# A hybrid decoder step on one core: another order of the prologue (root table, tile scaling, first weights, first projection)

## The chip, the cores and the metric

The kernel is one program on one core of a Trainium2 chip. The core has five engines that run their own instruction streams and meet at semaphores: TensorE (PE in the rows; PEld is its weight load), VectorE (DVE), ScalarE (ACT), GpSimd (POOL) and SyncE (SP), which here only issues transfers. The metric is the device time of one execution in microseconds (us), as the median of several runs.

## The reference, cut to what matters

One inference step of a one-layer decoder on 512 prompt tokens and 8 sample tokens, all in fp32. What the first microseconds of the kernel compute is this:

```python
h = rmsnorm(x, norm_mix_pre)          # x * rsqrt(mean(x*x) + EPS) * g, D_MODEL = 1024
z = einsum('btd,de->bte', h, w_in)    # queries, K/V of three branches, gates, S5 input u, merge gates
q, kv, gn, u, gm = split(z)
dt = exp(s5_log_dt); a_bar = exp((s5_a_re + 1j * s5_a_im) * dt)      # per S5 group and state
b_bar = ((a_bar - 1) / lam) * b_c                                    # then a scan over time with a_bar
```

The rest of the layer (sparse attention over a paged cache, the S5 recurrence, merge, MLP) follows and is the same in both kernels.

## The kernel before, in words

The tokens form four tiles of 128 rows and one of 8 (tile index 4, TT in the code), 520 columns in all once transposed (NT), handled in halves of 260 (HALF). The normalised input is kept transposed in hT, as 8 blocks of 128 channels by 520 tokens.

**SyncE** issues, in this order, the identity part of the constants (L726), the four prompt tiles of 512 KB (L728), the sample rows (L729), the rest of the constants (L730, 303 KB) and then the stream plan: slab 0 is w_in's 512 columns of the S5 input, 2 MB in one transfer (L784), followed by small_loads (L734 to L738: s5_d, s5_b_glu, the page table), then slab 1 in eight transfers (L803), state_load (L743) which waits until all five tiles are scaled, slab 2, and so on. A slab buffer is one of three.

**ScalarE** first issues five small loads (L1021 to L1024: the S5 parameters, then the two gain vectors), spreads log_dt over a tile (L1026), takes the exponential of dt (L1029), and then for each of the five token tiles does a Square with a row sum (L1016) and a Sqrt (L1009). Exp, Sin and Sin of the S5 angles follow (L1035 to L1037), then the loads of the C matrices (L1040) and a long zero fill (L1042).

**TensorE** transposes the S5 parameters and the gains, then in norm_transposes (through tp, L2153) each scaled tile in two halves of four 128-column blocks, into four PSUM banks in turn. It waits until all ten half tiles are evacuated (`xnt_free` at 10) and starts the units of the projection. A gemm unit (L2175) is one block of 128 output channels: for each half of the tokens, 8 matmuls of 260 columns. An fp32 matmul shows as two instructions, so a unit has 32. Units alternate between two pairs of PSUM banks, and ScalarE evacuates them (L1085). The order of the units is fixed in HEAD_UNITS and REST_UNITS: u0, u1, two of transposed C matrices ("ct"), u2, "kk", "ft" and "kt" units of S5, u3, q6, h0, then `chunk_ends(0)` (L2287), q7, and so on. chunk_ends(0) waits for `tables_done`, for ScalarE's chunk copies, and for the pair_free of the "ft" units.

**VectorE** copies parameters and gains out of PSUM, computes the S5 angle (L1451 to L1458), which ends with `ang_ready`, and then in input_norm takes for each tile the reciprocal of the root (L1436), scales the tile (L1439) into one of two buffers, and evacuates the transposes of the tile before with the gain multiplied in (L1429). After the last evacuation it waits for `trig_ready` from ScalarE and computes the S5 tables: L1461 to L1478 (a_bar and the coefficient of B), L1493 to L1500 (B with powers, `bb_ready`), L1513 to L1518 (tables of powers by doubling), and raises `tables_done` after the last L1518.

**GpSimd** zero-fills two areas (L874, L875), issues four small loads of the B matrices (L878), waits for `unit_ready` from VectorE, and computes powers of a_bar and products with C from there on.

## Time and profile before

| what | value |
|---|---|
| median of 3 runs | 1288.23 us (1286.51 to 1292.34) |
| the profiled execution's own time | 1290.65 us |
| its span, first to last instruction | 1288.9 us |
| mean granted TensorE clock | 0.983 of full |
| busy TensorE, weight load, VectorE, ScalarE, GpSimd | 95%, 78%, 64%, 24%, 26% |
| HBM read, written | 159.29 MB, 13.84 MB |

All views are of one profiled execution; times are microseconds from the first instruction. In a timeline, a row has the start, the length, the engine, the line of the kernel, the operation, out<-in, how many were merged, and in brackets the idle time ahead of it and what released it. Rows of the issuing queues (SPq, ACTq) are the time of the issue, not of the transfer. In the table of stretches, a row has from:to, its length, then busy us and count of instructions of PE, PEld, DVE, ACT and POOL in that order, then the granted TensorE clock (1.00 is full), the DMA share and GB/s. In the table of groups, a row has count, busy us, mean ns of one, and idle time before. DMA rows end with the median us from issue to landing.

### The profile page before, as it was taken

How to read it: one execution, taken by the hardware profiler on the slowest of the kernel's cores; microseconds unless marked ns; L12 is line 12 of the kernel's file. 1: busy time of each engine (PE TensorE's matmuls, PEld its weight loads, DVE VectorE, ACT ScalarE, POOL GpSimd, SP SyncE). 2: the span in 40 equal slices, each digit the busy share in tenths (PEclk: the TensorE clock that was granted, in tenths of full speed). 3: DMA queues.
4: the chain of work that ended last, by engine and by line, in shares of the span. 5: the costliest groups of instructions: out<-in, count | busy, mean ns of one | idle time of the engine just before them, and what ended most of it. 6: DMA issues, size and time to landing. Idle time of an engine off the chain costs nothing.

```text
span 1288.9 us, 20454 instructions
## 1 busy us (share of the span) xinstructions
PE 1226.6 (95%) x7778; PEld 1003.0 (78%) x7778; DVE 825.0 (64%) x1376; ACT 307.2 (24%) x728; POOL 337.9 (26%) x404
## 2 busy tenths in 40 slices
PE   5999899999999789999999999998999999999997
PEld 4888776668887556656788888887888888888886
DVE  6997332227888777877766554776664565467455
ACT  5485110120010465556311111132000000000002
POOL 5943224312221032223112111000211212513540
PEclk9999998899999999999999999998999999999999
DMA  9234445537777344434661322420231131131101
GB/s 256 50 132 135 164 110 173 163 108 311 261 261 258 114 117 135 157 97 151 221 203 66 114 78 103 177 103 17 74 122 66 66 131 66 66 131 66 66 1 67
DMA packets 122097, 166.09 MB, mean 129 GB/s; under 512 B 36448, under 2 KB 90528, under 8 KB 117648
## 3 DMA queue, kind: packets, MB, share of 16 engines
q1 hardware_dynamic: 103408, 104.72, 25.7%
q0 software_dynamic: 8080, 50.58, 10.9%
q10 hardware_dynamic: 10512, 9.49, 2.2%
q8 instruction: 62, 1.02, 0.3%
q14 instruction: 35, 0.29, 0.1%
HBM read 159.29 MB, written 13.84 MB: 134 GB/s over the span
## 4 chain that ended last, share of the span: by engine, by line
PE 86%; DVE 8%; ACT 3%; issue 2%; another core or an unknown queue 1%; DMA 0%; POOL 0%; ACTq 0%; DVEq 0%
PE PS L2623 47%; PE PS L2175 14%; PE PS L2352 9%; PE PS L2153 4%; PE PS L2304 2%; PE PS L2469 2%; PE PS L2501 2%; DVE small L1843 2%; PE PS L2534 1%; DVE PS L1841 1%; DVE R L1863 1%; ACT KVU L1136 1%; PE PS L2331 1%; PE PS L2287 1%
## 5 line engine op out<-in xcount | busy, mean ns | idle before, releaser
L2175 PE MATMUL PS<-hT,stream 128*128 128x260 f32 (+1 forms) x800 | 187.4, 395 | 5.1 <-ACT QO L1085 3.6
L2175 PEld LDWEIGHTS PS<-hT,stream 128*128 128x128 f32 (+1 forms) x800 | 153.2, 194 | 37.1 <-issue 4.9
L2623 PE MATMUL PS<-R,stream 128*128 128x260 f32 x752 | 173.5, 382 | 0.0
L2623 PEld LDWEIGHTS PS<-R,stream 128*128 128x128 f32 x752 | 142.8, 190 | 21.9
L2623 PE MATMUL PS<-R 128*128 128x260 f32 x592 | 135.7, 383 | 0.0
L2623 PEld LDWEIGHTS PS<-R 128*128 128x128 f32 x592 | 112.1, 190 | 17.8 <-DVE R L1895 0.8
L2352 PE MATMUL PS<-R 128*128 128x256 f32 (+1 forms) x544 | 119.0, 379 | 3.8 <-DVE R L1667 2.4
L2352 PEld LDWEIGHTS PS<-R 128*128 128x128 f32 x544 | 101.4, 194 | 18.5 <-DVE R L1667 2.8
L2623 PE MATMUL PS<-R,QO 128*128 128x260 f32 x496 | 113.8, 383 | 1.4 <-DVE QO L1895 1.4
L1983 DVE TENSOR_TENSOR R<-PS,R 128x260 f32<-128x260 f32 x100 | 42.4, 426 | 102.8 <-PE PS L2623 101.6
L2623 PEld LDWEIGHTS PS<-R,QO 128*128 128x128 f32 x496 | 93.8, 190 | 16.8 <-DVE QO L1895 2.2
L1983 DVE TENSOR_TENSOR KVU<-PS,KVU 128x260 f32<-128x260 f32 x92 | 39.2, 426 | 95.3 <-PE PS L2623 88.2
L2623 PE MATMUL PS<-hT,stream 128*128 128x260 f32 (+2 forms) x408 | 98.1, 384 | 0.6 <-ACT R L1290 0.6
L1667 DVE STREAM_TRANSPOSE R<-stream 128x2048 f32<-128x2048 f32 (+1 forms) x34 | 75.2, 2233 | 19.5 <-PE PS L2304 9.8
L2623 PEld LDWEIGHTS PS<-hT,stream 128*128 128x128 f32 x408 | 77.5, 196 | 12.4 <-ACT R L1290 0.8
L936 POOL DMA_INDIRECT R<-in_cache_kv_slc,row_kv x56 | 54.1, 966 | 110.3 <-DVE R L1619 65.9
L1619 DVE STREAM_TRANSPOSE R<-R 128x2048 f32<-128x2048 f32 x14 | 32.0, 2302 | 79.0 <-PE PS L2304 78.1
L2153 PEld LDWEIGHTS PS<-consts,R 128*128 128x128 f32 (+3 forms) x465 | 50.4, 141 | 40.8 <-issue 33.4
L1330 ACT ACTIVATE R<-PS 128x260 f32<-128x260 f32 x50 | 19.4, 388 | 251.2 <-PE PS L2623 251.2
L710 POOL TENSOR_SCALAR R<-R,small 128x512 f32<-128x512 f32 (+3 forms) x64 | 48.3, 758 | 116.6 <-DVE small L1850 116.6
L2153 PE MATMUL PS<-consts,R 128*128 128x128 f32 (+3 forms) x465 | 64.6, 279 | 11.9 <-DVE R L1863 7.2
L1273 ACT ACTIVATE R<-PS,small 128x512 f32<-128x512 f32 (+3 forms) x128 | 66.0, 527 | 9.2 <-DVE small L1843 8.3
(450 smaller groups left out, 1864.5 us busy)
## 6 DMA issues: line engine op xcount, KB each, us to landing
stream<-in_cache_kv_slc SPq DMA_DIRECT2D x128, 128.0 KB, 2.1
stream<-in_w_mlp_up SPq DMA_DIRECT2D x8, 2048.0 KB, 7.9
stream<-in_w_mlp_down SPq DMA_DIRECT2D x8, 2048.0 KB, 7.9
stream<-in_w_in SPq DMA_DIRECT2D x4, 2048.0 KB, 9.4
stream<-in_state_kv_win SPq DMA_DIRECT2D x16, 512.0 KB, 6.0
stream<-in_w_in SPq DMA_DIRECT2D x8, 1024.0 KB, 7.9
out_kv_win_sample<-in_state_kv_win POOLq DMA_DIRECT2D x1, 8176.0 KB, 43.3
R<-in_cache_kv_slc SPq DMA_DIRECT2D x56, 128.0 KB
```

The costliest lines, as they stand in the source:

```text
L710: return eng.tensor_scalar(S, S, ainv[:, k:k + 1], gtm[:, t, col:col + 1], ALU.mult, ALU.mult)
L936: pool.indirect_dma_start(key_pages(k)[:, x, :], None, slc_rows, bass.IndirectOffsetOnAxis(ap=row_kv[:, at:at + 1], axis=0)).then_inc(keys ...
L1273: ins = nc.scalar.activation(PP[:, n % 2, j, c0:c0 + P * (t + 1)], score_block(n, j, c0), ACT.Exp, bias=amx[:, k:k + 1], accum_out=asm[:, ...
L1619: V.transpose(KT[k % 2], KL[key_buffer(k)]).then_inc(kt_ready, 1)
L1667: V.transpose(ROWST[:, w % 3, 0:256 * ns].rearrange("p (s x) -> p s x", x=256), slab(s)[:, 0:512 * ns].rearrange("p (s k x) -> p k s x", k ...
L1843: V.reduce_max(amx[:, k:k + 2 * nx], S[:, :, 0:P * (t + 1)], AX, negate=True).then_inc(as_max, 1)
L1983: V.tensor_tensor(to, product_of(w, i), other, ALU.add).then_inc(pr_added, 1)
L2153: return nc.tensor.transpose(out, in_, ident[0:rows, 0:rows])
L2175: ins = M(pair(u)[0:w, hf, 0:HALF], lhs[k], rhs[k][:, HALF * hf:HALF * hf + HALF], start=(k == 0), stop=(k == n - 1))
L2304: ins = M(PS[32 * g:32 * g + 32, 4 + a4, cols], QM[rows, 256 * b + c0:256 * b + c0 + 32], keys[rows, :, c0:c0 + 32], start=(k == 0 and dh ...
L2352: ins = M(out, w1c[:, kind, x, :], rhs, start=(x == 0), stop=(x == 7))
L2623: ins = M(product_of(w, i)[:, c0:c1], lhs[:, k, :], rhs[:, k, c0:c1], start=(k == 0), stop=(k == nk - 1))
```

## The change

Five things change, all ahead of the second unit of the projection. The load of the Sqrt table and the root of tile 0 come ahead of the S5 parameters, and the gain vectors' loads ahead of the parameters'. GpSimd scales tiles 1, 3 and 4, VectorE keeps 0 and 2; the reciprocals stay on VectorE. Slab 0 comes in two transfers of 256 of its 512 columns, and the first is issued once tile 0 has landed, ahead of the rest of the constants. TensorE does the first unit, u0, in parts: the first 256 token columns (tiles 0 and 1) in two halves of the contraction, one ahead of the transposes of tile 3 and one ahead of those of tile 4, and the rest when all tiles are evacuated; the low half of the token columns is 260 wide, so four columns come by themselves. VectorE's S5 angle moves behind the evacuation of tile 2.

```diff
         def _(sp):
...
             sp.dma_start(xtm[0:NB, TT, :], a["x_sample"].rearrange("b o d -> (b o) d")).then_inc(x_in[TT], 16)
+            sp.wait_ge(x_in[0], 16)
+            sp.dma_start(slab(0).rearrange("p (k c) -> p k c", c=512)[:, :, 0:256],
+                         a["w_in"].rearrange("(k p) c -> p k c", p=P)[:, :, C_U:C_U + 256]).then_inc(x_in[0], 16)
             sp.dma_start(consts[:, P:CO_N], a["consts"][:, P:CO_N]).then_inc(masks_in, 16)
...
             def state_load():
-                sp.wait_ge(xn_ready, TT + 1)
+                sp.wait_ge(xn_ready, 2)
+                sp.wait_ge(xg_ready, 3)
...
-                    sp.dma_start(S[:, 0:KD * w].rearrange("p (k c) -> p k c", c=w),
-                                 wq[:, :, c0:c0 + w]).then_inc(done, 16)
+                    c1 = 256 if n == 0 else 0
+                    sp.dma_start(S[:, 0:KD * w].rearrange("p (k c) -> p k c", c=w)[:, :, c1:w],
+                                 wq[:, :, c0 + c1:c0 + w]).then_inc(done, 16)
...
         def _(pool):
...
+            for k, t in enumerate((1, 3, TT)):
+                r = ROWS[t]
+                pool.wait_ge(gains_ready, 2 + k)
+                if t >= 2:
+                    pool.wait_ge(xnt_full, 2 * (t - 1))
+                nc.gpsimd.tensor_scalar(xn[0:r, t % 2, :], xtm[0:r, t, :], rstd[0:r, t:t + 1], None,
+                                        ALU.mult).then_inc(xg_ready, 1)
             pool.wait_ge(unit_ready, 1)
...
         def _(act):
...
+            for w, name in enumerate(("norm_mix_pre", "norm_mlp_pre")):
+                act.dma_start(gnat[KD * w:KD * w + KD, :], a[name].rearrange("(k p) -> k p", p=P)).then_inc(gains_in, 16)
             for k, name in enumerate(("s5_a_re", "s5_a_im")):
                 act.dma_start(nat[:, k, :], a[name].rearrange("(i g) n -> i (g n)", g=2)).then_inc(par_in, 16)
             act.dma_start(ldt2, a["s5_log_dt"].rearrange("(i g) -> i g", g=2)).then_inc(par_in, 16)
-            for w, name in enumerate(("norm_mix_pre", "norm_mlp_pre")):
-                act.dma_start(gnat[KD * w:KD * w + KD, :], a[name].rearrange("(k p) -> k p", p=P)).then_inc(gains_in, 16)
+            act.wait_ge(eps_ready, 1)
+            nc.scalar.activation(preload, epsb, ACT.Sqrt)
+            input_root(0)
             act.wait_ge(par_in, 16 * N_PAR)
             nc.scalar.activation(nat[:, 2, :].rearrange("p (g n) -> p g n", g=2),
                                  ldt2.unsqueeze(2).to_broadcast([NST, 2, N5]), ACT.Copy).then_inc(nat_ready, 1)
+            for t in range(1, TT + 1):
+                input_root(t)
             act.wait_ge(par_ready, 1)
             nc.scalar.activation(dt, ldt, ACT.Exp).then_inc(ldt_ready, 1)
-            act.wait_ge(eps_ready, 1)
-            input_roots()
...
         def _(dve):
...
-            dve.wait_ge(par_full, 1)
-            V.tensor_copy(par3, PS[:, 0, 0:3 * NST]).then_inc(par_ready, 1)
             dve.wait_ge(gains_full, 1)
             V.tensor_copy(gflat, PS[:, 1, 0:2 * KD]).then_inc(gains_ready, 1)
             dve.wait_ge(gains_ready, 1)
+            norm_scale(0)
+            norm_inverse(1).then_inc(gains_ready, 1)
+            dve.wait_ge(par_full, 1)
+            V.tensor_copy(par3, PS[:, 0, 0:3 * NST]).then_inc(par_ready, 1)
+            norm_evac(0)
+            norm_scale(2)
+            norm_inverse(3).then_inc(gains_ready, 1)
+            norm_evac(1)
+            norm_inverse(TT).then_inc(gains_ready, 1)
+            norm_evac(2)
             dve.wait_ge(ldt_ready, 1)
             V.tensor_tensor(mag, are, dt, ALU.mult)
...
             V.tensor_scalar(ang2, ang2, 3.1415925, -3.1415925, ALU.min, ALU.max).then_inc(ang_ready, 1)
-            input_norm()
+            norm_evac(3)
+            norm_evac(TT)
             dve.wait_ge(trig_ready, 1)
...
+            def first_unit(part):
+
+                S = slab(0).rearrange("p (k c) -> p k c", c=512)
+                bank = pair(0)[:, 0, :]
+                if part < 2:
+                    for k in range(4 * part, 4 * part + 4):
+                        M(bank[:, 0:2 * P], S[:, k, 0:P], hT[:, k, 0:2 * P], start=(k == 0), stop=(k == KD - 1))
+                    return
+                for k in range(KD):
+                    M(bank[:, 2 * P:HALF], S[:, k, 0:P], hT[:, k, 2 * P:HALF], start=(k == 0), stop=(k == KD - 1))
+                for k in range(KD):
+                    ins = M(pair(0)[:, 1, 0:HALF], S[:, k, 0:P], hT[:, k, HALF:NT], start=(k == 0), stop=(k == KD - 1))
+                ins.then_inc(pair_full, 1)
+
             pe.wait_ge(consts_in, 16)
+            pe.wait_ge(gains_in, 32)
+            tp(PS[:, 1, 0:2 * KD], gnat, 2 * KD).then_inc(gains_full, 1)
+            norm_transposes(0)
             pe.wait_ge(par_in, 16 * N_PAR)
...
             ins.then_inc(par_full, 1)
-            pe.wait_ge(gains_in, 32)
-            tp(PS[:, 1, 0:2 * KD], gnat, 2 * KD).then_inc(gains_full, 1)
-            norm_transposes()
+            norm_transposes(1)
+            norm_transposes(2)
+            pe.wait_ge(xnt_free, 4)
+            pe.wait_ge(x_in[0], 32)
+            first_unit(0)
+            norm_transposes(3)
+            first_unit(1)
+            norm_transposes(TT)
             pe.wait_ge(xnt_free, 10)
+            first_unit(2)
...
-                    wait_slab(pe, n)
+                    if to != ("u", 1):
+                        wait_slab(pe, n)
...
             for u, unit in enumerate(UNITS):
-                projection(u, unit)
+                if u:
+                    projection(u, unit)
```

norm_transposes(t) is the body of the old loop for one tile, with xn_ready for tiles 0 and 2 and xg_ready for 1, 3 and 4. norm_scale(t) is norm_inverse(t) and the old scaling. A later wait on xn_ready (L2648) counts 3 fewer.

## Rows read from the trace of the kernel before

**Rows 1.** The page: busy time and share of TensorE.

```profile
PE 1226.6 (95%) x7778; PEld 1003.0 (78%) x7778; DVE 825.0 (64%) x1376; ACT 307.2 (24%) x728; POOL 337.9 (26%) x404
```

**Rows 2.** Timeline of TensorE, 0 to 160 us.

```profile
8.45 0.28 PE L2153 MATMUL PS<-consts,QO 16*128 16x16 f32 x1 [0.82 <-DMA QO<-in_norm_mlp_pre]
...
17.47 1.09 PE L2153 MATMUL PS<-consts,QO 128*128 128x128 f32 x8 [0.96 <-DVE QO L1439]
...
20.90 15.98 PE L2175 MATMUL PS<-hT,stream 128*128 128x260 f32 x64 [0.73 <-DVE hT L1429]
...
70.14 3.71 PE L2287 MATMUL PS<-QO,R 128*128 128x136 f32 x16 [2.43 <-issue]
...
144.20 15.98 PE L2175 MATMUL PS<-hT,stream 128*128 128x260 f32 x64 [3.56 <-ACT QO L1085]
```

**Rows 3.** Timeline of VectorE, from 11 and from 69 us.

```profile
11.00 0.75 DVE L1439 TENSOR_SCALAR QO<-KVU,small 128x1024 f32<-128x1024 f32 x1
...
20.77 0.15 DVE L1461 TENSOR_TENSOR small<-small 128x16 f32<-128x16 f32 x1
...
69.27 0.68 DVE L1518 TENSOR_TENSOR R<-R,KVU 128x512 f32<-128x512 f32 x1
```

**Rows 4.** Table of stretches (columns as told above).

```profile
10.50:11.00 0.50, 0.00 (x0) 0.00 (x0) 0.16 (x2) 0.50 (x2) 0.00 (x0) 1.00 0.95 180
...
20.77:69.95 49.18, 45.28 (x270) 38.21 (x270) 46.96 (x119) 23.36 (x30) 43.59 (x90) 0.97 0.51 130
...
22.30:25.70 3.40, 3.40 (x9) 2.67 (x8) 2.96 (x20) 2.70 (x1) 2.63 (x13) 0.50 1.18 263
...
70.20:73.50 3.30, 3.30 (x15) 3.30 (x16) 2.70 (x6) 3.23 (x6) 2.17 (x3) 0.51 0.16 52
...
145.20:148.40 3.20, 3.20 (x9) 2.52 (x8) 2.97 (x18) 0.00 (x0) 0.00 (x0) 0.50 1.00 348
```

**Rows 5.** Timeline of ScalarE.

```profile
8.03 1.04 ACT L1016 ACTIVATE QO<-KVU 128x1024 f32<-128x1024 f32 x1
...
9.18 1.28 ACT L1009 ACT_TABLE_LOAD   x1
...
17.77 1.28 ACT L1036 ACT_TABLE_LOAD   x1
...
29.90 0.60 ACT L1085 ACTIVATE KVU<-PS 128x520 f32<-128x520 f32 x1 [4.91 <-PE PS L2175]
...
143.54 0.60 ACT L1085 ACTIVATE QO<-PS 128x520 f32<-128x520 f32 x1 [9.71 <-remote]
```

**Rows 6.** Timeline of SyncE's queue, 0 to 40 us.

```profile
1.20 1.84 SPq L728 DMA_DIRECT2D KVU<-in_x_prompt  x4
...
4.50 0.46 SPq L784 DMA_DIRECT2D stream<-in_w_in  x1
...
16.57 10.30 SPq L803 DMA_DIRECT2D stream<-in_w_in  x8
```

**Rows 7.** DMA issues: first prompt tile, fourth, rest of constants, slab 0.

```profile
KVU<-in_x_prompt SPq DMA_DIRECT2D x1, 512.0 KB, 5.1
...
KVU<-in_x_prompt SPq DMA_DIRECT2D x1, 512.0 KB, 9.4
...
consts<-in_consts SPq DMA_DIRECT2D x1, 303.0 KB, 10.6
...
stream<-in_w_in SPq DMA_DIRECT2D x1, 2048.0 KB, 15.3
```

**Rows 8.** Groups by shape: GpSimd's scaling, narrow and 256-column matmuls.

```profile
L710 POOL TENSOR_SCALAR R<-R,small 128x512 f32<-128x512 f32 x16 | 16.6, 1041 | 38.3 <-DVE small L1850 38.3
...
L710 POOL TENSOR_SCALAR R<-R,small 128x128 f32<-128x128 f32 x16 | 7.6, 484 | 16.0 <-DVE small L1850 16.0
...
L2352 PE MATMUL PS<-R 128*128 128x256 f32 x512 | 113.7, 381 | 2.7 <-DVE R L1667 2.4
...
L2623 PE MATMUL PS<-hT,stream 128*128 128x4 f32 x24 | 3.2, 263 | 0.0
```

More of the change, by code:

```diff
@@ L288, in build @@
         xn_ready = sem("xn_ready")
+        xg_ready = sem("xg_ready")
         xnt_full = sem("xnt_full")
@@ L861, in build @@
         N_PAR = 3
-        NORM_UNITS = [(t, half) for t in range(5) for half in range(2)]
         @block.gpsimd
@@ L1010, in root, with input_root @@
                                             bias=epsb[0:rows, :])
-            def input_roots():
-                for t, r in enumerate(ROWS):
-                    act.wait_ge(x_in[t], 16)
-                    link(nc.scalar.activation(junk[0:r, :], xtm[0:r, t, :], ACT.Square,
-                                              accum_out=ssq[0:r, t:t + 1]))
-                    root(t, t + 1, r).then_inc(root_ready, 1)
+            def input_root(t):
+                r = ROWS[t]
+                act.wait_ge(x_in[t], 16)
+                link(nc.scalar.activation(junk[0:r, :], xtm[0:r, t, :], ACT.Square,
+                                          accum_out=ssq[0:r, t:t + 1]))
+                root(t, t + 1, r).then_inc(root_ready, 1)
+            for w, name in enumerate(("norm_mix_pre", "norm_mlp_pre")):
+                act.dma_start(gnat[KD * w:KD * w + KD, :], a[name].rearrange("(k p) -> k p", p=P)).then_inc(gains_in, 16)
             for k, name in enumerate(("s5_a_re", "s5_a_im")):
@@ L2153, in tp, with norm_transposes @@
                 return nc.tensor.transpose(out, in_, ident[0:rows, 0:rows])
-            def norm_transposes():
-                for v, (t, half) in enumerate(NORM_UNITS):
-                    r = ROWS[t]
-                    pe.wait_ge(xn_ready, t + 1)
+            def norm_transposes(t):
+                r = ROWS[t]
+                if t in (0, 2):
+                    pe.wait_ge(xn_ready, 1 + t // 2)
+                else:
+                    pe.wait_ge(xg_ready, 1 + t // 2)
+                for half in range(2):
+                    v = 2 * t + half
                     if v >= 4:
@@ L2647, in norm_back @@
                 r, k0 = ROWS[t], (XN_AT[t] - 6) % 2
-                pe.wait_ge(xn_ready, XN_AT[t])
+                pe.wait_ge(xn_ready, XN_AT[t] - 3)
                 if t == TT:
```

38 lines of the change are left out of this document (18 added, 20 removed).

## The prediction

> **What bounds the kernel now.** I read the page first [rows 1]: TensorE (PE) is busy 95% of 1288.9 us, so a change of the start is worth what it shifts the later TensorE work, and no more. Then the order of TensorE's work [rows 2]: the first projection (channel tile u0) starts at 20.90, having waited 0.73 us for VectorE (DVE), and from there PE is almost solid until it sits idle for 2.43 us before 70.14 (so from 67.71). That idle decides the case. What starts at 70.14 is L2287, the first chunk_ends, which waits for tables_done; the view names no releaser ("issue"), but VectorE's order does [rows 3]: the last L1518 of the S5 tables runs from 69.27 to 69.95 and the increment follows it. Going back, this table chain starts at L1461 at 20.77, the instant the last norm evacuation (L1429) is over, and VectorE is busy 46.96 of the 49.18 us between [rows 4]. So two chains run from about 20.8 to 70.1: TensorE's, with 2.43 us of slack, and VectorE's, with none. After 70.14 TensorE never waits long again before 140.7; 144.20 has a wait of 3.56 us [rows 2] whose cause the trace doesn't name.
>
> An earlier start of TensorE alone is therefore worth nothing: it lengthens the 2.43 us. What counts is when VectorE can begin L1461.
>
> **The change, part by part.**
>
> Roots. Before, the first Square waits behind the parameter path and the Sqrt table load stands between it and its root: 8.03, load 9.18 for 1.28, first root finished 10.76 [rows 5]. Now the load runs right after the five DMA issues (about 3.05 to 4.4, under the wait for data; the load lasts the same 1.28). Tile 0 lands at 1.20 + 5.1 = 6.3 [rows 6, 7], Square 1.04 and its accumulator read 0.2, Sqrt 0.3: root 0 at 7.9, 2.9 us sooner. The parameter copy waits for the last of ScalarE's five small loads, 8.45 before [rows 2], then root 1 at 10.1, root 2 at 11.5. Tile 3 lands at 2.6 + 9.4 = 12.0 [rows 7], so root 3 is at 13.4 and the last at 14.7. Exp's table load and the exponential of dt follow: 16.2. One load of 1.28 goes, on an engine that isn't late: nothing.
>
> Scaling. VectorE's is 0.75 a tile [rows 3]. GpSimd's isn't shown at 1024 columns; its two-operation form takes 484 ns at 128 and 1041 at 512 [rows 8]: slope 1.45 ns a column, so 1.8 us at 1024. Bounds: 0.75 (VectorE's) and 2.1 (twice the 512). I take 1.8. GpSimd has nothing else queued before unit_ready but its four load issues, over before root 1. Tile 1: reciprocal 10.3, ready 12.2. Tile 2 on VectorE: 13.9. Tile 3: from 14.1, ready 15.9. Tile 4 follows: 17.8. Cover: TensorE, as next shown, isn't ready for tile 3 before 18.3 and for tile 4 before 21.1. If GpSimd took 2.4 us more a tile, tile 3 would begin to cost. The Trainium skill (GPSIMD Engine Reference, Engine selection) advises against elementwise work there, but puts one-input work at roughly line rate; an estimate by it is 0.9 us a tile at that page's 1.2 GHz. By either price the sum is the same.
>
> First weights. The whole slab was issued at 4.50 and landed at 19.8 [rows 6, 7]. Its first half is now issued once tile 0 is in (6.4). In the queue it stands where the 303 KB of constants stood, which landed at 4.11 + 10.6 = 14.7. So by 14.7 some 0.3 MB are in; 2.1 MB then took 5.1 us (0.41 MB/us), the other 0.75 MB take 1.8: first half in at 16.5. Bounds: 15.5, where it no longer matters since tile 1's evacuation ends there, and 19.8. The rest lands near 20, before it is needed. SP's issues behind it (s5_d, s5_b_glu, page table, the next slab at 16.57 [rows 6]) go back by 2.7 us. That slab, the vectors and the page table are first read by q6 behind u3, by VectorE's L1507 and by its L1547 behind the tables, each over 15 us after landing: nothing. The state load's wait (both scaling semaphores) is met by 17.8, sooner than SP reaches it. The c loads on ScalarE's queue move 1 us back and are needed only when u0 and u1 are through: nothing.
>
> TensorE, from 16.5. first_unit(0): 8 instructions (an fp32 matmul is two) of 256 columns at 0.222 [rows 8]: 1.8, to 18.3. Eight transposes of tile 3, 1.1 [rows 2]: 19.4. first_unit(1), 1.8: 21.2. Tile 4's transposes 0.7 and VectorE's two small evacuations 0.2: xnt_free is complete at 22.1. Then 16 instructions of 4 columns at 133 ns [rows 8] = 2.1, work that the old unit didn't have, and 16 of 260, 3.5: u0 ends at 27.7 at full clock. Before, it ended at 29.9 [rows 5].
>
> Clock. Each time that dense work follows a sparse stretch the granted clock is 0.50 (1.2 of 2.4 GHz) for over 3 us: 22.3 to 25.7, 70.1 to 73.5, 145.2 to 148.4 [rows 4]. It costs 1.7 us each time, and it came 0 to 1.4 us after the dense work began. The new dense work begins at 16.5, so the dip falls in first_unit(0) and (1), and the evacuations are complete at 23.8, u0 at 29.4. Without it, 22.1 and 27.7. I take it inside, by those three rows.
>
> VectorE. The angle chain now stands behind evacuation 2 (17.0): 1.4 us for its seven small operations gives 18.4. ScalarE's Exp, Sin load 1.28 and two Sins follow (before, 17.77 to 19.38 for the load and Sins) [rows 5]: trig ready 20.4. But norm_evac(3) and norm_evac(4) come before the trig wait in VectorE's order, and these wait for transposes which TensorE has put behind first_unit(0) and (1). So **a wait takes the removed one's place**: L1461's successor starts not at 20.77 but at 23.8. The late party is the first weights.
>
> **Sum.** VectorE's chain +3.0, carried rigidly (its waits in between are on GpSimd, which starts from the same unit_ready): tables_done at 73.1. TensorE gets there at 67.2, 0.5 sooner, and sits idle 5.9 instead of 2.43 us. The half-clock stretch behind it costs 1.85 as before. ScalarE's table copies and chunk copies move with VectorE's chain. All later work moves by +3.0: 1290.65 of the profiled execution would be 1293.7. That execution stands 2.4 above the median 1288.23, so against the median: **1291.2 us**. Bounds: the first half in by 15.5 and no dip, 21.1, is +0.3; landing at 19.8 with the dip is +6.3.
>
> **Rivals.**
> (a) The new wait is short: half slab by 15.5, dip missing or behind the evacuations. Shift 0.3 to 1.3, TensorE 1 to 3 us sooner at 67.7 and that wasted: 1288.5 to 1289.5. For it: between 10.5 and 11.0 all queues together moved only 180 GB/s [rows 4], with GpSimd's small loads among them; should these interleave less with SP's queue, the half is in sooner. Against: their order is not changed. A gain past 0 has no room in this case, since trig itself is ready at 20.4.
> (b) The unexplained 3.56 us at 144.20, with its dip of 1.7, goes or shrinks since everything before has moved: 1291.2 - 5.3 = 1285.9. For it: ScalarE resumes at 143.54 [rows 5] for an evacuation whose matmuls ended at 140.2, so it isn't a plain dependence. Against: it may move along.
> (c) Slower beyond the measurable: the first half slab lands where the whole one did or later (it is cut into 1 KB rows rather than 2 KB, and its issue waits for tile 0). Place: TensorE's wait for x_in[0] = 32; price: one us for each us behind 16.5. From 19.9 on the loss is over 6.4: 1294.7.
> (d) The split doesn't do what it says: u0 ends no sooner, since 2.1 us of narrow matmuls and the dip eat the start. That is nearly in the forecast, same time.
> The Trainium skill (SBUF — State Buffer, two separate sides) says that GpSimd and a VectorE operation with two SBUF inputs lock each other out. By it tile 4's scaling until 17.8 would hold the angle chain by up to 0.8, trig 21.2. That is hidden in the forecast; it would take case (a)'s lower end from 0.3 to 0.5.
>
> **How the numbers follow.** A measurement of this kernel tells about 0.5%, 6.4 us, from no change. Forecast and (d) 0.57, (a) 0.20, (b) 0.12, (c) 0.08; the rest 0.03 for a gain that I don't see. Faster needs under 1281.8: the rest and a little of (b), 0.04. Slower needs over 1294.7: (c) and a new unexplained wait, 0.08. Same 0.88. The range takes in (b) at 1285.5 and the forecast's own bounds to 1295.
>
> **What would show it.** Right: root 0 near 7.9; first L-line of the projection at 16 to 17, u0's evacuation near 29; the S5 chain's first operation (before L1461) at 22 to 24; the idle before the first chunk_ends 4 to 7 us and that start at 71.5 to 74; clock 0.50 between 16.5 and 23. Wrong: S5 chain begun before 20.8, chunk_ends before 70, or the projection begun before 15.

## The result, and the profile after

| | before | changed |
|---|---|---|
| median | 1290.76 us (1282.97 to 1294.03, 9 runs) | 1297.43 us (1289.77 to 1301.15, 9 runs) |
| ratio of the two | | 1.0051, 95% interval 1.0027 to 1.0075 |
| the profiled execution | 1290.65 us, span 1288.9 | 1301.15 us, span 1299.4 |
| mean granted clock of it | 0.983 | 0.977 |

The changed kernel is slower by 6.6 us (3.5 to 9.7, from the interval), where 1291.2 and a shift of +3.0 were forecast. Its 1297.43 lies outside the range on the slow side. The median of the kernel before is 2.5 higher here than the 1288.23 of three runs that the forecast stood on; from 1290.76 the same shift gives 1293.8, still 3.6 short. The lines of the page and the timelines of TensorE, GpSimd and VectorE in the changed kernel's prologue (a row: start, length, engine, line, operation, out<-in, and in brackets the idle time ahead and its releaser):

```profile
span 1299.4 us, 20485 instructions
PE 1236.4 (95%) x7794; PEld 1012.1 (78%) x7794; DVE 824.2 (63%) x1373; ACT 306.5 (24%) x728; POOL 347.0 (27%) x407
```

```profile
12.88 3.68 PE L2177 MATMUL PS<-consts,QO 128*128 128x128 f32 x16 [1.89 <-POOL QO L891]
16.63 2.69 PE L2219 MATMUL PS<-hT,stream 128*128 128x256 f32 x8
19.15 1.04 PE L2177 MATMUL PS<-consts,QO 128*128 128x128 f32 x8
20.03 1.89 PE L2219 MATMUL PS<-hT,stream 128*128 128x256 f32 x8
21.85 0.66 PE L2177 MATMUL PS<-consts,QO 8*128 8x8 f32 x8
22.79 1.95 PE L2222 MATMUL PS<-hT,stream 128*128 128x4 f32 x16 [0.28 <-DVE hT L1442]
24.59 5.44 PE L2224 MATMUL PS<-hT,stream 128*128 128x260 f32 x16
```

```profile
9.97 2.85 POOL L891 TENSOR_SCALAR QO<-KVU,small 128x1024 f32<-128x1024 f32 x1 [1.01 <-DVE small L1451]
15.03 5.65 POOL L891 TENSOR_SCALAR QO<-KVU,small 128x1024 f32<-128x1024 f32 x2 [2.21 <-PE PS L2177]
```

```profile
17.20 0.17 DVE L1474 TENSOR_TENSOR small<-small 128x16 f32<-128x16 f32 x1
...
17.93 1.05 DVE L1478 TENSOR_SCALAR small<-small 128x16 f32<-128x16 f32 x1
...
22.30 0.44 DVE L1442 TENSOR_TENSOR hT<-PS,small 128x32 f32<-128x32 f32 x2 [1.22 <-PE PS L2177]
22.65 0.17 DVE L1485 TENSOR_TENSOR small<-small 128x16 f32<-128x16 f32 x1
```

These rows show the replaced wait. L1485 is the operation that was L1461, and it starts at 22.65 where it started at 20.77 [rows 3], straight behind the two small evacuations of tile 4 (L1442), which waited 1.22 us for transposes that stand behind both parts of the first unit. That is 1.88 us, and it is carried from there. TensorE's later stops in the changed kernel, and ScalarE's evacuations that released two of them ("remote" stands where the profile finds no instruction that ended just before the signal):

```profile
72.07 3.36 PE L2339 MATMUL PS<-QO,R 128*128 128x136 f32 x16 [4.19 <-DVEq L1565]
...
120.81 8.79 PE L2203 MATMUL PS<-hT,stream 128*128 128x260 f32 x32 [2.63 <-ACT QO L1100]
...
150.41 9.85 PE L2203 MATMUL PS<-hT,stream 128*128 128x260 f32 x36 [3.56 <-ACT QO L1100]
```

```profile
120.15 0.60 ACT L1100 ACTIVATE QO<-PS 128x520 f32<-128x520 f32 x1 [8.93 <-remote]
...
149.76 0.60 ACT L1100 ACTIVATE QO<-PS 128x520 f32<-128x520 f32 x1 [9.72 <-remote]
```

The first chunk_ends (72.07, before 70.14 [rows 2]) is 1.93 later. The stop at 150.41 is that of 144.20 [rows 2], 6.2 later and the same 3.56 long. Between them lies the stop at 120.81, which the kernel before does not have: ScalarE begins at 120.15 to evacuate a unit whose last matmul ended near 115.4 (TensorE's next group, L2306, starts at 115.23), so the unit's `pair_full` reached it nearly 5 us late. 1.93 of the shift thus comes from the prologue and 4.3 from this stop (2.63) and the half-clock stretch behind it (1.7). Together 6.2, against 6.6 measured. The two profiled executions differ by more, 10.5, and what they differ by over 6.2 comes behind 250. It goes with the clock: (1 - clock) x span is 29.9 us in the changed one and 21.9 in the other, and 0.977 is on the low side of that kernel's runs.

### The profile page after: what moved, and what is told of

It is laid out like the page before. It is cut to its first block, busy times and chain, and to the rows that moved or that the text cites. A ratio compares the mean times of both kernels' runs of the same rounds, so it can differ in the third digit from the quotient of the medians.

```text
span 1299.4 us, 20485 instructions
## 1 busy us (share of the span) xinstructions
PE 1236.4 (95%) x7794; PEld 1012.1 (78%) x7794; DVE 824.2 (63%) x1373; ACT 306.5 (24%) x728; POOL 347.0 (27%) x407
## 4 chain that ended last, share of the span: by engine, by line
PE 82%; DVE 10%; ACT 3%; issue 2%; another core or an unknown queue 1%; POOL 1%; DMA 0%; ACTq 0%; DVEq 0%
PE PS L2676 46%; PE PS L2203 10%; PE PS L2405 9%; PE PS L2177 5%; PE PS L2356 2%; PE PS L2522 2%; PE PS L2554 2%; DVE small L1867 2%; PE PS L2587 1%; ACT KVU L1151 1%; DVE PS L1865 1%; DVE R L1887 1%; PE PS L2384 1%; PE PS L2559 1%
## 5 line engine op out<-in xcount | busy, mean ns | idle before, releaser
L2203 PE MATMUL PS<-hT,stream 128*128 128x260 f32 (+1 forms) x768 | 180.4, 395 | 7.0 <-ACT QO L1100 6.2
L2203 PEld LDWEIGHTS PS<-hT,stream 128*128 128x128 f32 (+1 forms) x768 | 147.4, 194 | 38.2 <-ACT QO L1100 6.7
L2676 PEld LDWEIGHTS PS<-R,stream 128*128 128x128 f32 x752 | 142.8, 190 | 21.9
L2405 PE MATMUL PS<-R 128*128 128x256 f32 (+1 forms) x544 | 121.9, 386 | 4.4 <-DVE R L1691 2.4
```

What stands on the lines that cost most here:

```text
L2203: ins = M(pair(u)[0:w, hf, 0:HALF], lhs[k], rhs[k][:, HALF * hf:HALF * hf + HALF], start=(k == 0), stop=(k == n - 1))
L2405: ins = M(out, w1c[:, kind, x, :], rhs, start=(x == 0), stop=(x == 7))
L2676: ins = M(product_of(w, i)[:, c0:c1], lhs[:, k, :], rhs[:, k, c0:c1], start=(k == 0), stop=(k == nk - 1))
```

## The experiments

Ratios are to the kernel before on the same chip in the same minutes, and "by the ratio" means the ratio times that kernel's median; it can differ from the difference of the medians by up to 2.4 us. The "offset" at a place is how much later TensorE starts a piece of work than in the profiled execution before. The experiments ran on different chips: on one the kernel before takes 1289 us (chip A; e1, e2, e6, e7 and e13 to e16), on others 1264 (chips B: e3, e4, e5, e8 to e12, e17, e18). The first measurement, at 1290.76, looks like A, and its two traces have the late signals of A.

**VectorE alone late (e1), TensorE's program alone longer (e2).**

```diff
# e1: the kernel before, behind input_norm()
+            for _ in range(2):
+                link(V.memset(junk, 0.0))
# e2: the kernel before, behind pe.wait_ge(xnt_free, 10)
+            for k in range(KD):
+                M(pair(0)[:, 0, 0:4], ident, hT[:, k, 0:4], start=(k == 0), stop=(k == KD - 1))
```

> The kernel before, with nothing changed but VectorE's S5 table chain, which two memsets of an unused 128x1024 area (about 0.9 us each) hold back by 1.9 us, as the change did (22.65 against 20.77). Theory A: the whole measured loss is this delay, in two steps. The first chunk_ends moves from 70.14 to 72.0 (+1.9); and since TensorE's work then stands about 2 us later against the GpSimd gathers and SyncE's key issues, the late signal behind the pair evacuated near 118 now stops TensorE (idle 2 to 3 us and a half-clock stretch), so that the offset behind 124 is +5 to +7 and the time +6 us. Theory B (the second step comes from TensorE's 16 added instructions or from something else in the changed prologue): offset +1.9 at 72 and still +1.9 at 124, time +2 us, no idle of TensorE above 1 us near 120. Theory C (the second step is chance of one execution): the same as B in most executions.

> The kernel before, with 8 matmuls of 4 columns (16 instructions, about 2 us; what they write is overwritten) on TensorE right ahead of the first unit of the projection. TensorE has 2.43 us of idle ahead of 70.14, so the first chunk_ends stays at 70.1 with 0.4 us of idle ahead of it. Theory A (only a shift of the work behind 70 against GpSimd's gathers counts): offset 0 everywhere behind 70, time +0 (within 1 us). Theory B (the place of TensorE's code in its fetches, 16 instructions further as in the changed kernel, makes the late signal near 118 stop TensorE): chunk_ends at 70.1, and a new idle of 2 to 3 us near 118 to 120 with its half-clock stretch, offset +4 behind 124, time +4 us.

Measured: e1 1292.22 against 1289.09, ratio 1.0017 (0.9999 to 1.0035), which is +2.2 us with 0 just inside the interval. e2 1288.24, ratio 0.9993 (0.9971 to 1.0015). TensorE's first chunk_ends and the late signal in e1:

```profile
71.97 3.96 PE L2289 MATMUL PS<-QO,R 128*128 128x136 f32 x16 [3.85 <-issue]
```

```profile
116.24 0.61 ACT L1085 ACTIVATE QO<-PS 128x520 f32<-128x520 f32 x1 [4.18 <-PE PS L2177]
121.30 4.45 ACT L1136 ACTIVATE KVU<-PS 32x512 f32<-32x512 f32 x4 [4.45 <-remote]
```

So the first step is shown: VectorE's delay alone moves chunk_ends by 1.8. The second is not what theory A said. The projection unit is evacuated on time (116.24), the next signal, of a short unit, is late, and nobody on TensorE waits for it: no stop near 120. In e2 there is none either. So neither the delay nor the longer program brings the stop by itself, and theory A, which put the whole loss on the delay, fell.

How large the first step is, one pair of traces can't tell. The prologue of the kernel before varies by some 1.3 us between executions: without added work on VectorE its table chain starts at 19.46 to 20.77 in six traces (before, e2, e7, e10, e16, e17), and the 20.77 that all is measured from is the latest. The changed kernel's starts at 21.70 to 22.65 in six (changed, e6, e9, e11, e13, e14). The means, 19.96 and 22.10, are 2.1 apart, where the one pair gives 1.9.

**GpSimd's gathers taken away early on (e7 before, e6 changed; again in e16).** The same edit in each, with VectorE's waits to match:

```diff
-                    for x in range(0, 8, 2):
+                    for x in (range(8) if k < 7 else range(0, 8, 2)):
...
-            for k in range(NKU):
+            for k in range(7, NKU):
                 wait_key_buffer(pool, k)
```

> The kernel before, with the key pages of key units 0 to 6 all fetched by SyncE's direct loads (8 issues a unit in place of 4), so that GpSimd's first gathers come only with key unit 7. Theory A with its cause (signals of TensorE reach ScalarE late while GpSimd's gathers and SyncE's issues run against each other): no wait of ScalarE of over 3 us put down to a remote signal between 105 and 150 where its matmuls were long over; the 3.56 us idle of TensorE at 144.20 and its half-clock stretch (1.7 us) gone, so about 5 us sooner behind 150, time -5 us, if SyncE's loads keep up with VectorE. Rival: the late signals come from SyncE's issues or from TensorE's own instruction fetch, and stay: time 0 or slower, if the keys come late.

> The changed kernel, with the same shift of the key pages of units 0 to 6 from GpSimd's gathers to SyncE's direct loads. Theory A with its cause: both late signals (ScalarE waiting until 120.15 and until 149.76 for matmuls long over) are gone; TensorE's offset to the kernel before stays +1.9 from 72 to the end, less what the wait at 144 gave: against the same edit on the kernel before +2 us and not +6.6, time about 1288. Rival (the gathers are not the cause): the stop at 120.8 stays, and the time is that of the changed kernel, 1297, or more.

Measured: e7 1282.48, ratio 0.9945 (0.9922 to 0.9968); e6 1287.43, ratio 0.9969 (0.9943 to 0.9994). Neither trace has a late signal; in e7 the evacuation that waited until 143.54 [rows 5] follows its matmuls at once:

```profile
137.61 0.60 ACT L1085 ACTIVATE QO<-PS 128x520 f32<-128x520 f32 x1 [6.41 <-PE PS L2176]
```

That settles that on chip A the late signals come with GpSimd's gathers of key pages (8 in a row from about 107, 12 from about 127, one each 1.25 us): SyncE's loads alone, now twice as many, hold nothing. But the changed kernel, so treated, is still slower than the kernel before, so treated: by 3.1 us by the ratios, by 4.95 by the medians. The times can't tell that from my "+2"; the traces can. The projection unit that starts at 138.27 in e7 starts at 141.88 in e6, 3.6 later. 1.93 of it is the first chunk_ends. The rest is clock: ahead of chunk_ends TensorE is idle 2.46 us in e7 and 4.19 in e6; the group of 16 takes 2.09 in the one and 3.73, at half clock, in the other:

```profile
69.33 2.09 PE L2288 MATMUL PS<-QO,R 128*128 128x136 f32 x16 [2.46 <-issue]
```

```profile
71.26 3.73 PE L2340 MATMUL PS<-QO,R 128*128 128x136 f32 x16 [4.19 <-DVEq L1565]
```

**Both delays (e8), and the parts of the change taken back (e3, e4, e5).** e8 has the edits of e1 and e2. e3 is the changed kernel with the first unit whole:

```diff
-            pe.wait_ge(xnt_free, 4)
-            pe.wait_ge(x_in[0], 32)
-            first_unit(0)
             norm_transposes(3)
-            first_unit(1)
             norm_transposes(TT)
             pe.wait_ge(xnt_free, 10)
-            first_unit(2)
+            pe.wait_ge(x_in[0], 32)
+            wait_slab(pe, 0)
+            gemm(0, ...).then_inc(pair_full, 1)
```

e4 is the changed kernel with GpSimd's loop over (1, 3, TT) gone and `norm_scale(1)`, `norm_scale(3)`, `norm_scale(TT)` on VectorE in the places of `norm_inverse`; there the last one stands behind norm_evac(2). e5 has both edits.

> The kernel before with both earlier edits: VectorE's table chain held back by 1.9 us, and 16 narrow instructions more on TensorE ahead of the first unit. Theory D (the second step of the loss needs both: the shift of 1.9 us against GpSimd's gathers and a program of TensorE that is longer ahead of them, which puts its instruction fetch near 116 right behind the end of a unit whose signal is then late): chunk_ends at 72, a unit's evacuation near 120 that waits for a remote signal for 8 to 9 us, TensorE idle 2 to 3 us there, offset about +6 behind 124, time +6 us. Rival E (it is neither of these two but something else in the changed kernel, or chance): offset +2 behind 124, time +2 to +3, as with the delay alone (1292.22 against 1289.09).

> The changed kernel, but the first unit is one piece again behind all transposes (32 instructions, no 4-column matmuls). GpSimd's scaling of tile 4, over at 20.7, is then what VectorE waits for: its table chain starts at 22.0 (22.65 in the changed kernel, 20.77 before), chunk_ends at 71.3. Theory D: TensorE's program is as long as before ahead of the gathers, so no second stop near 120; offset +1.2 from 72 on, time +1 to +2 us against the kernel before. Rival E: a shift of over 1 us is enough: second stop near 120, offset +5, time +5 or more. If the interleave alone made the first step of the loss, the table chain would start at 20.8 instead.

> The changed kernel, but VectorE scales all five tiles and GpSimd none; the interleaved first unit stays. TensorE is solid from the landing of the first half slab (16.6) to the transposes of tile 4 (22.5), so the table chain starts at 22.3 to 22.7 as in the changed kernel (22.65), chunk_ends at 71.7 to 72.1: the interleave is by itself enough for the first step. Theory D: the second stop near 120 comes too, time +5 to +7 against before. Rival: GpSimd's slow scaling (2.83 us a tile) makes the delay; then the chain starts at 21 or sooner, chunk_ends at 70.2, time +0.

> The changed kernel with both taken back: VectorE scales all tiles, and the first unit is one piece behind all transposes. What is left of the change is the root table first, the split slab and the order of the small loads. Roots 3 and 4 end at 12.5 and 13.9, so all evacuations end by 19; the angle chain (1.4 us), one table load (1.28) and two Sins then set the start of the table chain: 20.5 to 21.0, against 20.77 before. chunk_ends at 69.9 to 70.4, no second stop near 120, time -1 to +1 us against before. If it came out at +2 us or more, a part that I hold harmless (the split slab, the order of the loads) costs something.

These came on a chip B, where the kernel before takes 1264.06 and no trace has a late signal, so they say nothing of the stop near 120. They measure the first step. The table puts them beside e10 and e11, the two kernels unchanged on another chip B. Its last column but one is the time from the start of the first chunk_ends to the start of the projection unit near 140, between which TensorE is almost never idle:

| kernel | table chain starts | idle, then length of the first chunk_ends | from there to the unit near 140 | median; ratio |
|---|---|---|---|---|
| e10, before | 19.84 | 2.75; 2.65 | 70.66 | 1264.20; 1.0006 (0.9990 to 1.0022) |
| e5, neither | 20.21 | 1.70; 2.09 | 68.95 | 1264.58; 1.0005 (0.9989 to 1.0020) |
| e4, VectorE scales | 20.98 | 5.87; 3.97 | 71.49 | 1269.84; 1.0038 (1.0018 to 1.0057) |
| e3, no interleave | 21.87 | 1.31; 2.09 | 68.93 | 1266.70; 1.0008 (0.9992 to 1.0024) |
| e11, changed | 21.78 | 4.15; 3.47 | 70.63 | 1268.71; 1.0032 (1.0015 to 1.0050) |
| e8, both delays | 21.98 | 1.68; 2.09 | 68.94 | 1267.86; 1.0028 (1.0012 to 1.0045) |

Each part is by itself enough for a delay of the table chain, against e10: the interleave (e4) for 1.1 us, GpSimd's scaling (e3) for 2.0. These are single traces and good to about 1 us, since the chain of the kernel before varies as told; e3's start lies outside that range by 1.1 and e4's by 0.2, and for both the waits in the trace name the cause. They do not add, because TensorE and GpSimd run side by side. In e4 TensorE waits for the half slab, and the transposes of tile 4 stand behind that:

```profile
15.68 1.97 PE L2207 MATMUL PS<-hT,stream 128*128 128x256 f32 x8 [1.11 <-DMA stream<-in_w_in]
```

In e3 the last evacuation waits for the transposes of a tile that GpSimd hands over at 20.66:

```profile
15.01 5.65 POOL L891 TENSOR_SCALAR QO<-KVU,small 128x1024 f32<-128x1024 f32 x2 [2.20 <-PE PS L2177]
```

With both taken back (e5) the loss is gone within 0.2%: the early table, the split slab and the order of the small loads cost nothing that shows, and bring nothing.

The column of the unit near 140 shows a second cost. Eight traces without late signals (e3, e5, e7, e8, e9, e12, e16, e17) have no half clock behind the first chunk_ends and take 68.93 to 68.97 us; four (e6, e10, e11, e18) have a stretch of it and take 70.61 to 70.66; e4, after the longest idle of them, takes 71.49. So the stretch costs 1.7 us of TensorE's time, and more in e4. That is why e4, whose chain starts 0.8 sooner than the changed kernel's, is at the unit near 140 no sooner (141.89 for 141.80). The times of whole executions are too noisy to show as much: e8, with neither a long idle nor the stretch, has nearly the ratio of e11, and the intervals of e3, e4, e8 and e11 all overlap.

**The two kernels again on one chip, both delays again, and the idle filled (e10, e11, e12, e9).**

```diff
# e9: the changed kernel, in chunk_ends(0)
                     pe.wait_ge(pair_free, U_FT + 1)
+                    for k in range(8):
+                        M(PS[:, 4, 0:HALF], ident, hT[:, k, 0:HALF], start=(k == 0), stop=(k == 7))
                     pe.wait_ge(tables_done, 1)
```

> The kernel before, unchanged, so that its trace stands beside the others on one chip. The second set of experiments ran on a chip on which this kernel takes 1264 us and no trace has a late signal. Where the time is near 1290, I expect the late signals at 118.4 and 143.5 with the stop of TensorE at 144.2 again; where it is near 1264, neither. In both, an idle of TensorE of 1.7 to 2.5 us ahead of 70, and the half-clock stretch behind it in some executions only.

> The changed kernel, unchanged, on the same chip as the other three. Theory F (the loss has up to three terms: VectorE's table chain 1.9 us later on every chip; the half-clock stretch of 1.7 us behind the first chunk_ends in all executions and not only in some, since TensorE's idle ahead of it grows from 2.4 to over 4 us; and, only on a chip with late signals, the stop near 120 for 4.2 us): near 1290 the ratio to before is +6 to +8 us; near 1264 it is +2 to +5 us, with chunk_ends at 72 and no stop near 120. Rival G (one term of 1.9 and the rest clock chance): +2 us on both.

> The kernel before with VectorE's chain 1.9 us later and 16 narrow instructions more on TensorE, once more, for a chip with late signals. There, theory D (stop near 120 by the shift and the longer program together) gives a stop of 2 to 3 us near 120 and an offset of about +6 behind 124; if the offset stays +2, program length and shift are not what decides and the choice of the late signal stays open. On a chip without late signals: +2 to +4 us as before (1267.86 against 1264.06).

> The changed kernel with 8 matmuls of 260 columns (16 instructions, about 3.5 us; what they write is overwritten) on TensorE ahead of its wait for tables_done, in the idle time before the first chunk_ends. Theory F: TensorE stays busy until about 71.3, the granted clock stays 1.00 behind 72 (in the changed kernel 3.4 us at 0.50), and the kernel is 1.5 to 1.9 us faster than the changed kernel. If idle time ahead does not set the clock, the half-clock stretch stays and the time is that of the changed kernel. The filler also lengthens TensorE's program by 32 entries ahead of the gathers: on a chip with late signals the stop near 120 may move or go.

Again a chip B (1263.67). e11: 1268.71, ratio 1.0032, +4.0 us by the ratio, with chunk_ends at 71.17 for 69.22 (+1.95) and no late signal. e12: 1266.34, ratio 1.0022 (1.0006 to 1.0037). e9: 1266.47, ratio 1.0026 (1.0013 to 1.0039), 2.2 us under e11's median and 0.8 by the ratios. Its TensorE around chunk_ends, and the stretch behind it in e11 and in e9 (columns as in the stretches shown ahead; the clock is the third figure from the end):

```profile
66.76 3.67 PE L2333 MATMUL PS<-hT,consts 128*128 128x260 f32 x16
71.06 2.12 PE L2341 MATMUL PS<-QO,R 128*128 128x136 f32 x16 [0.62 <-DVEq L1565]
```

```profile
71.20:74.60 3.40, 3.40 (x17) 3.40 (x18) 3.04 (x7) 3.31 (x7) 2.25 (x4) 0.57 0.15 44
```

```profile
71.20:74.60 3.40, 3.40 (x24) 3.20 (x25) 3.04 (x8) 3.31 (x7) 2.26 (x4) 1.00 0.21 60
```

Work thrown into the idle keeps the granted clock at 1.00 (2.4 GHz) where it was 0.57 on average (mostly 1.2 GHz), and TensorE is at the unit near 140 at 140.03 where it was there at 141.80. That gain of 1.8 us in the traces is what shows the mechanism. That the whole kernel is faster by it is not shown: the intervals of the two ratios overlap. In all 20 traces of this case, with 3.85 us or more of idle ahead of the first chunk_ends, its 16 instructions took 3.10 to 3.97 us in 7 of 7; with 2.75 or less they took 2.09 to 2.12 in 10 of 13, and longer in before, e10 and e18. Theory F fits the traces on both kinds of chip. Rival G's +2 is just inside e11's interval (1.9 to 6.3 us), and the stretch is what speaks against it.

**For the stop near 120, on chip A once more (e14 changed, e15 both delays, e13 with fewer narrow matmuls and so four token columns of the first unit left incomplete, e16 = e7).**

```diff
# e13: the changed kernel, in first_unit(2)
-                for k in range(KD):
-                    M(bank[:, 2 * P:HALF], S[:, k, 0:P], hT[:, k, 2 * P:HALF], start=(k == 0), stop=(k == KD - 1))
+                M(bank[:, 2 * P:HALF], S[:, 0, 0:P], hT[:, 0, 2 * P:HALF], start=True, stop=True)
```

> The changed kernel, unchanged. Near 1290 (a chip with late signals) the stop of TensorE near 120 comes again (idle 2 to 3 us, offset about +6 behind 124) and the ratio is +5 to +8 us if that stop is of the kernel; if it was chance of one execution, no stop and +2 to +5 us. Near 1264: no stop, +4 to +5 us as before.

> The kernel before with VectorE's chain 1.9 us later and 16 narrow instructions more on TensorE. On a chip with late signals theory D says a stop near 120, offset +6 and +6 us; rival: offset +2 and +2 to +4 us. On another chip +3 us as twice before.

> The changed kernel with 1 of the 8 four-column matmuls (four token columns of the first unit are then sums over 128 channels instead of 1024). TensorE's program is 14 instructions shorter, within 2 of the kernel before, and the first unit ends 1.7 us sooner, which lengthens the idle ahead of the first chunk_ends (72.0 as in the changed kernel) to about 5.9 us. On a chip with late signals theory D says no stop near 120: offset +1.9 there, 4 us faster than the changed kernel. Rival (the program's length does not matter): the stop stays. On another chip: the time of the changed kernel within 1 us, since the 1.7 us are wasted in the idle.

> The kernel before with the key pages of units 0 to 6 loaded by SyncE and not gathered by GpSimd. On a chip with late signals -6.6 us as in its first measurement. On a chip without them there is nothing to win at 118 and 143: 0, or up to 2 us slower if SyncE's 16 loads in a row make the keys late.

Measured, against 1288.88: e14 1297.09, ratio 1.0067 (1.0041 to 1.0092, 4 runs); e15 1291.87, ratio 1.0024 (1.0004 to 1.0043); e13 1293.56, ratio 1.0034 (1.0015 to 1.0053); e16 1283.55, ratio 0.9957 (0.9940 to 0.9973). The changed kernel's stop is there again, in e14, 2.61 us for 2.63:

```profile
120.03 0.60 ACT L1100 ACTIVATE QO<-PS 128x520 f32<-128x520 f32 x1 [8.89 <-remote]
```

```profile
120.69 8.95 PE L2203 MATMUL PS<-hT,stream 128*128 128x260 f32 x32 [2.61 <-ACT QO L1100]
```

In e15 the same signal is late by some 2 us and TensorE doesn't have to wait for it; in e13 it is later, and TensorE stops 1.30:

```profile
115.63 0.60 ACT L1085 ACTIVATE QO<-PS 128x520 f32<-128x520 f32 x1 [6.11 <-remote]
```

```profile
119.04 7.28 PE L2203 MATMUL PS<-hT,stream 128*128 128x260 f32 x32 [1.30 <-issue]
```

So the stop is of the changed kernel on that chip and not chance. Theory D failed in both its forecasts: e15 has the shift and the longer program and no stop, e13 has the shorter program and a stop. Its yes or no is a more or less in the traces, by how much the unit's signal is late: 0 (e1, e2, before), 2 (e15), 3.5 (e13) and 5 us (e14, changed). SyncE, which issues eight loads beside the first eight gathers, is often slow too. Its rows in the kernel before, the changed kernel and the changed kernel on chip B:

```profile
107.19 8.95 SPq L771 DMA_DIRECT2D R<-in_cache_kv_slc  x8
```

```profile
109.18 12.51 SPq L776 DMA_DIRECT2D R<-in_cache_kv_slc  x8
```

```profile
108.29 8.21 SPq L776 DMA_DIRECT2D R<-in_cache_kv_slc  x8
```

The eight take 8.25 in e1, 11.24 in e2, 11.40 in e13, 12.34 in e14 and 12.48 in e15, so SyncE is slow wherever the unit's signal is late, and in e2 too, where it isn't. One order fits the seven traces of chip A with this burst of eight gathers: where the unit ended before the sixth gather began, its signal was on time (before: 113.24 and 113.35; e1, e2); where it ended after, the signal was late (changed: 115.23 and 114.91; e13, e14, e15), and the further behind, the later: 0.01 us behind (e15) 2 us late, 0.23 (e13) 3.5, 0.3 (e14, changed) nearly 5. It was found in the traces afterwards and no run tested it; on chip B the unit of e11 ends 0.3 behind (114.34 and 114.02) and its signal is on time. The unit ends 6.57 us behind the first gather in both kernels (106.67 and 108.66); it is the first gathers that took longer in before. In the burst of twelve the order doesn't hold. In the kernel before and in the changed one the held signal comes 1.1 to 1.2 us after the end of the burst's last gather (117.37 and 118.44; 118.93 and 120.15), as if it waited for the burst; in e15 the unit's signal comes before that. What makes one burst slow and another not, on one chip and with the gathers equally spaced, stays open.

**Is there a version faster than both? (e17 = e7, e18 = e5 with the edit of e7.)**

> The kernel before with the key pages of units 0 to 6 loaded by SyncE and not gathered by GpSimd. On a chip near 1289: -5 to -7 us as twice before. On a chip near 1264, where no signal is late: 0, since all that it takes away are late signals; slower by 1 to 2 us if SyncE's 16 loads in a row make keys late.

> The same, and with what is left of the change without its two costs: root table first, split first slab, other order of the small loads; all tiles scaled by VectorE, first unit in one piece behind all transposes. VectorE's table chain starts at 20.5 to 21.2 as in the kernel before, so against e17 it is 0 within 1 us: the early roots are not worth anything, since the angle chain and the Sin table set the start of the tables. If it is over 1.5 us slower than e17, one of these parts costs something that I hold for free.

On a chip B (1263.91): e17 1264.28, ratio 1.0007 (0.9994 to 1.0020); e18 1265.63, ratio 1.0002 (0.9988 to 1.0016). So the loads on SyncE cost nothing where no signal is late, and save 5.5 and 7.1 us (by the ratios of e16 and e7) where signals are. The kernel before with that edit is the best version tried on chip A, and level with the kernel before on B. Of the change nothing adds to it: e18's table chain starts at 19.66, 0.2 sooner than e10's, and no time comes of it.

## Why the prediction was wrong

**What held.** VectorE's chain has no slack and TensorE's has: TensorE is ready for the first chunk_ends at 67.88 (before 67.71), VectorE 1.93 later than before, and the idle ahead of it grew from 2.43 to 4.19. "A wait takes the removed one's place", at norm_evac(4) behind the first unit: shown by e4. Root 0 was due at 7.9 and its Sqrt ended at 7.47; the first half slab was due at 16.5 and landed then, 10.5 after its issue at 6.00:

```profile
stream<-in_w_in SPq DMA_DIRECT2D x1, 1024.0 KB, 10.5
```

The unit began at 16.63. But "the late party is the first weights" is half of it: the transposes of tiles 1 and 2, which had waited 1.89 us for GpSimd's first scaling, ended only at 16.56, so that the start would have been the same with earlier weights. That the two fall together is luck. u0's evacuation was due near 29 and started at 30.07, no sooner than before (29.90). So rival (d), "u0 ends no sooner", came true, and the early first unit gained TensorE nothing. (a) and (c) did not happen, nor did (b), the stop at 144 going away: it moved along.

**Sizes within the chain.** The table chain was due at 23.8 and came at 22.65, chunk_ends at 73.1 and came at 72.07, its idle at 5.9 and it was 4.19. The half-clock stretch that I had put inside first_unit(0) and (1) began only at 24.9, in the rest of the unit:

```profile
24.90:28.30 3.40, 3.40 (x9) 2.62 (x8) 2.99 (x22) 2.52 (x1) 2.55 (x12) 0.50 1.13 255
```

That took 1.7 off my sum, and first_unit(0), 2.69 for 1.8, gave 0.9 back. The profile shows a granted clock of 1.00 there, but the same eight matmuls took 1.89 at 20.03, and transposes too were slow until then (16 in 3.68 from 12.88, 8 in 1.04 from 19.15). A lower clock that the profile doesn't show would fit, and is not shown. GpSimd's scaling was the worse miss: 1.8 us a tile with bounds 0.75 to 2.1, from its 128- and 512-column operations [rows 8], and it took 2.83. "If GpSimd took 2.4 us more a tile, tile 3 would begin to cost" left out that tile 3 cannot start before its buffer is free (15.03, not 14.1), so that tile 4 is done only at 20.68. In the changed kernel the first unit still covers that, and TensorE takes tile 4 at 21.85; but e3 shows that GpSimd's scaling alone delays the chain by 2.0 on a chip B, about as much as the whole change. The Trainium skill (GPSIMD Engine Reference, Engine selection) puts one-input work at roughly line rate, an estimate of 0.9 us at that page's 1.2 GHz; the trace disagrees by a factor of three. The measurement decides.

By the Trainium skill's page SBUF — State Buffer (two separate sides) I had estimated that GpSimd's scaling holds VectorE's angle chain by up to 0.8 us. The trace agrees in size: L1478 took 1.05 for 0.17 and trig was ready at 21.47 (21.2 by that estimate), still hidden behind 22.65. It disagrees on which operation: L1474, with two inputs from SBUF, ran in 0.17 while GpSimd scaled tile 3. And it disagrees on how long: by that section the pair of ports is held for the whole instruction, yet L1478 ended at 18.98, in the middle of GpSimd's scaling of tile 4 (until 20.68).

**The step that failed** is the last of the sum: "TensorE [...] sits idle 5.9 instead of 2.43 us. The half-clock stretch behind it costs 1.85 as before. [...] All later work moves by +3.0." It assumed twice that what follows 70 is rigid. First, the stretch "as before" was in the one execution I had; of the five traces with 2.4 to 2.8 us of idle (before, e7, e10, e16, e17) two have it, and with 3.85 or more all seven have it. The longer idle, which I had booked as free, makes a half-clock stretch of 1.7 us from a chance into what looks like certainty. How much of the time of whole executions this is stays open. The mean clock can't tell: (1 - clock) x span, averaged over the runs, is 12.2 us before, 15.1 in e11 and 13.4 in e9, but also 14.7 in e12, whose trace has full clock behind chunk_ends and half clock at 20 to 27 (0.55 on average), inside TensorE's slack. Second, and larger, on chip A a unit's signal that was on time before arrives 5 us late where TensorE needs it: 4.3 us with its half-clock stretch. The unit stands as far behind the first gather as before (6.57 us), and the same shift in e1 brings no stop, so "everything moved" is not the reason; which property of the changed kernel is, stays open. I had read the late signal at 143.54 as "unexplained" and let it go away or move along; a second one at 118.44 stood in the trace of before, costing nothing, and the prediction doesn't mention it:

```profile
118.44 4.43 ACT L1136 ACTIVATE KVU<-PS 32x512 f32<-32x512 f32 x4 [4.40 <-remote]
```

With 1.9 for the chain (2.1 by the means of six traces) and 4.3 for the stop the sum would have been +6.2, and the measured +6.6 and +8.6 (e14) hold it within their intervals (3.5 to 9.7 and 5.3 to 11.9). On chip B, where there is no stop, the changed kernel loses 4.0 (1.9 to 6.3), which the forecast's +3.0 fits. That is luck: the chain came 1.1 us short of its +3.0, and the half clock, booked at no change, made up for it. The prediction left 0.08 for "(c) and a new unexplained wait", too little for a cause whose trace was in hand.

## What to carry to other kernels

Before costing an earlier start, find which of the converging chains has slack, and price the idle that the other one gains: in this case a pause of 3.85 us or more was followed by a half-clock stretch of 1.7. Filling the pause with work kept the clock up in the one trace that tried it. A wait whose signal comes long after the work that it waits for ("remote") is a hazard that a small change can move onto the critical path; take its cause away first (here, GpSimd's gathers), and read also those that cost nothing now.

## What was not expected of the hardware

- The same kernel takes 1289 us on one chip and 1264 on others. On the first, signals of TensorE reach ScalarE 2 to 5 us late during bursts of GpSimd gathers (118.44, 143.54), on the others never (eight traces with gathers), with gathers spaced alike (1.25 us). The late signals explain some 5 to 7 us of the 25 (e7, e16); the rest lies mainly between 180 and 290 and was not studied.
- GpSimd's multiplication by a per-partition scalar costs 2.83 us at 128x1024 where VectorE takes 0.75 [rows 3], and meanwhile a 16-column VectorE operation takes 1.05 for 0.17.
- A pause of TensorE of 3.85 us or more ahead of the first chunk_ends was followed by half clock in 7 of 7 traces, and of 2.75 or less in 3 of 13. Ahead of the unit near 145 on chip A the pause is 3.56 to 3.61 in seven traces, and five go on at half clock, e1 and e15 at full. In e15 (pause 3.61):

```profile
144.60:148.00 3.40, 3.40 (x16) 2.96 (x17) 3.17 (x18) 0.57 (x4) 0.00 (x0) 1.00 0.85 248
```
